# ScalarE alternates exponentials and copies in the wide steps of the second mixer's attention

## The reference

```
score = where(causal, score, -inf);  _, sel = top_k(score, 256)
sc = where(valid, einsum(qa, c_sel), -inf)
p  = softmax(sc);  o_lat = einsum(p, c_sel);  return einsum(o_lat, w_uv)
```

## Time and profile before

| | us |
|---|---|
| median of three runs | 2987.97 |
| lowest, highest | 2983.38, 2990.4 |
| the profiled execution | 2987.91 |
| its span | 2986.1 |
| TensorE busy in it | 2840.4 |
| VectorE busy | 2155.3 |
| ScalarE busy | 1311.8 |
| GpSimd busy | 185.9 |

### The profile page before, as it was taken

The page is one execution under the profiler, slowest core; times in us unless marked ns, Lnnn a source line. Parts: engine busy times, 40 slices in busy tenths (PEclk is TensorE's granted clock), DMA queues, the critical chain, the costliest instruction groups (busy, mean ns, idle before and its releaser), DMA issues.

```text
span 2986.1 us, 37449 instructions
## 1 busy us (share of the span) xinstructions
PE 2840.4 (95%) x13573; PEld 2267.0 (76%) x13573; DVE 2155.3 (72%) x3933; ACT 1311.8 (44%) x2305; POOL 185.9 (6%) x203
## 2 busy tenths in 40 slices
PE   7998997999999999999999999998899899999997
PEld 4885676788888887788888886685567778888886
DVE  7888637988888567766665675998747866665568
ACT  3124744544444554433333442477654433333443
POOL 2050000000000000000000000123520000000000
PEclk9988998999999999999999999999999999999999
DMA  6542033244446773345447762111024244455864
GB/s 229 164 133 38 9 134 120 81 163 162 162 162 208 264 253 113 128 162 162 162 162 283 231 194 74 36 43 34 1 83 137 95 162 162 151 163 186 300 196 147
DMA packets 345414, 436.84 MB, mean 146 GB/s; under 512 B 29685, under 2 KB 191517, under 8 KB 345054
## 3 DMA queue, kind: packets, MB, share of 16 engines
q1 hardware_dynamic: 342274, 428.46, 43.9%
q10 hardware_dynamic: 2956, 5.99, 0.6%
HBM read 317.59 MB, written 116.50 MB: 145 GB/s over the span
## 4 chain that ended last, share of the span: by engine, by line
PE 79%; DVE 13%; ACT 3%; DMA 2%; issue 2%; POOL 1%; SPq 0%; DVEq 0%; ACTq 0%
PE psum L1991 37%; PE psum L1442 21%; PE psum L2865 5%; PE psum L1082 5%; PE psum L1982 3%; DVE count_junk L3375 1%; DMA ada_piece<-in_w_ada 1%; PE psum L4183 1%; PE psum L3055 1%; ACT probs L498 1%; DMA ada_w<-in_w_ada 1%; PE psum L4091 1%; DVE x_t L1688 1%; PE psum L3068 1%; DVE ada_acc L3903 1%
## 5 line engine op out<-in xcount | busy, mean ns | idle before, releaser
L1442 PE MATMUL psum<-far_op,far_op 128*128 128x512 f32 x2772 | 629.4, 389 | 0.0
L1442 PEld LDWEIGHTS psum<-far_op,far_op 128*128 128x128 f32 x2772 | 520.1, 188 | 107.9
L1991 PE MATMUL psum<-x_b,w_near 128*128 128x512 f32 x1440 | 346.2, 389 | 0.8 <-DVE w_near L1614 0.8
L1991 PE MATMUL psum<-x_t,w_near 128*128 128x512 f32 x1440 | 337.1, 389 | 2.3 <-ACT psum L1728 2.3
L1991 PE MATMUL psum<-x_t,w_far 128*128 128x512 f32 x1440 | 336.3, 389 | 0.0
L1991 PEld LDWEIGHTS psum<-x_t,w_near 128*128 128x128 f32 x1440 | 270.0, 188 | 59.6 <-ACT psum L1728 3.6
L1991 PEld LDWEIGHTS psum<-x_b,w_near 128*128 128x128 f32 x1440 | 270.5, 188 | 57.5 <-issue 1.2
L1991 PEld LDWEIGHTS psum<-x_t,w_far 128*128 128x128 f32 x1440 | 270.2, 188 | 56.5 <-ACT u_keep L1740 0.4
L1213 DVE TENSOR_TENSOR far_op<-far_a,far_op 128x512 fp32r<-128x512 f32 x231 | 160.6, 695 | 175.3 <-ACT far_op L1206 173.8
L1206 ACT CAST far_op<-far_a 128x512 fp32r<-128x512 f32 x231 | 143.9, 623 | 315.9 <-PE psum L1442 307.7
L1991 PE MATMUL psum<-x_b,w_far 128*128 128x512 f32 x720 | 176.3, 394 | 9.1 <-DVE val_row L1860 9.1
(11 more groups left out here) (516 smaller groups left out, 4861.3 us busy)
## 6 DMA issues: line engine op xcount, KB each, us to landing
far_a<-row_ops SPq DMA_DIRECT2D x231, 256.0 KB, 2.9
row_ops<-hidden SPq DMA_DIRECT2D x99, 512.0 KB, 5.6
raw<-in_ffn_w SPq DMA_DIRECT2D x88, 512.0 KB, 4.5
col_sums<-hidden SPq DMA_DIRECT2D x66, 512.0 KB, 5.7
far_b<-col_sums SPq DMA_DIRECT2D x132, 256.0 KB, 3.3
raw<-in_w_up SPq DMA_DIRECT2D x44, 512.0 KB, 3.9
hidden<-in_ffn_w SPq DMA_DIRECT2D x44, 512.0 KB, 5.2
far_b<-in_ffn_w SPq DMA_DIRECT2D x66, 256.0 KB, 3.2
```

The source lines that it names most:

```text
L1442: ins = t.matmul(bank(b + n), l[slot][:, rows], r[slot][:], start=(fresh and i == 0 and m == 0), stop=(i == FH - 1 and m == 2), skip_group ...
L1991: ins = t.matmul(bank(b), at[:, l, cols], x[:, k, r], start=(start and k == 0 and m == 0), stop=(k == 3 and m == 2), skip_group_check=not ...
```

## The change

In the loop over the wide steps the exponential of item 2j is put before the copy of item 2j-2. Nothing is added or taken away, and no other engine's list is touched.

```
         for j in range(NARROW, PAIRS2):
+            exponentials(2 * j)
             copy_probs(2 * j - 2)
-            for i in (2 * j, 2 * j + 1):
-                exponentials(i)
+            exponentials(2 * j + 1)
             last_of(j)
             copy_probs(2 * j - 1)
             if j == EARLY_SPLIT:
```

## The result

| | before | changed |
|---|---|---|
| median, us | 2986.40 | 2993.39 |
| lowest, highest, us | 2980.15, 2991.86 | 2990.68, 2997.55 |
| runs | 17 | 17 |
| changed over before | | 1.0026, 95% interval 1.0019 to 1.0032 |
| span of the profiled execution, us | 2986.1 | 2988.9 |

The changed kernel is slower by 0.26%, some 7.8 us of 2986 (5.7 to 9.6 by the interval; the two medians differ by 7.0). The two spans differ by only 2.8 us, less than the ratio says. They are one execution each, and before the change's first effects they already lay apart: the first turn of step 16, ahead of anything that the change can reach, began at 2119.80 us in the one and at 2115.02 in the other. So the traces are compared here over a stretch, from the start of step 17 to the start of the last turn (item 63): 86.37 us before, 93.82 changed, 7.45 more.

A forecast was written before the change was run, and what follows sets the result against it. TensorE's own list was taken to bound an ordinary wide step, with ScalarE having slack. Step terms from -0.5 to +2.3 us summed to 7.65, say +7.6, on 2987.91 us: 2995.5 us, range 2990.0 to 2999.5.

The forecast's parts named there:

- What bounds: An ordinary wide step is as long as TensorE's own list; the first copy has 0.41 us to spare.
- Ordinary steps: First copy late for the second turn: steps 18, 19 +1.4; 22, 23 +1.4; 28 +0.95; 29 +0.7; 30, 31 +1.5 us.
- Steps 20 and 24: Behind VectorE's selection, 0.7 us of delay goes into TensorE's waits for GpSimd of 2.30 and 2.49 us: 0.
- Step 21: Maximum done early, so the first copy is in time, and a 0.46 us wait behind a block's output goes: -0.5 us.
- Steps 16 and 17: Start of the wide steps, where TensorE waits for GpSimd and a copy anyway: -0.1 us together, an estimate.
- Step 25: Second turn late anyway, as TensorE's values took 2.83 us instead of 1.53: 0.
- Steps 26 and 27: Step 27's copy stands behind an exponential held up by VectorE's remainders of the casts: +2.3 us for both steps.
- The clock: A shorter pause after step 24 and a new 3.1 us pause in step 27 were let cancel; bounds -1.4 and +3.
- the rival of a falling clock: Clock falls once or twice more, after step 27's 3.1 us pause; one slow stretch gives 9.2, 2997.1 us; chance 0.20.
- The table: More changes between exponential and copy on ScalarE bring no table load: 0; a load at each would cost 41 us.
- Only half of it arrives: Step 25's slow stretch goes, and recovery at steps 16 to 21 or hidden delays leave about 4.8 us: 2992.7; chance 0.25.
- Faster: Step ends hang on ScalarE's second copy behind two exponentials; relief gives -1.6 us in all, 2986.3; chance 0.05.

The follow-up runs named there:

- the first experiment, wait: Kernel of before, plus a one-column copy waiting for the step's own maximum ahead of each wide step's first copy; 2990.88 us, ratio 1.0014.
- the dose: Kernel of before with VectorE's remainders behind step 27's reciprocals and five one-column copies ahead of each wide step's first copy; 2989.09 us, ratio 1.0008.
- the selection experiment: Kernel of before with the changed order in steps 20, 21, 24 and 25 alone; 2983.51 us, ratio 0.9989.
- not27: Changed kernel, but step 27 keeps the order of before; 2990.09 us, ratio 1.0014 against before.
- rest+: Changed kernel with VectorE's remainders of the casts moved behind step 27's reciprocals; 2989.86 us, ratio 1.0011 against before.
- the seventh experiment: Kernel of before with only VectorE's remainders of the casts moved behind step 27's reciprocals; 2984.14 us, ratio 0.9993.
- shifted: Kernel of before with each wide step's second exponential put behind its second copy; 2989.44 us, ratio 1.0011.

## Why the prediction was right

Forecast 2995.5 us, +7.6, against a ratio that means +7.8, and +7.45 in the traced stretch. The median measured is 2993.39, 2.1 lower than forecast: 1.6 of that is the kernel of before, whose median over 17 runs is 2986.40 and not 2987.97. The mechanism was right, and the terms that belong to it came to 0.1 us in nearly every step. That the sum agrees to some tenths is in part luck: from step 16 on, where the traces differ by 7.64 us, the order of the list accounts for 6.8, and 0.8 us of clock, put at nothing, made up the rest.

- *What bounds.* TensorE's own list, with 0.41 us of cover for the first copy: shown by the first experiment (a copy 0.28 us later costs nothing) and the dose.
- *Ordinary steps.* 0.70 each expected at 640 and 768 keys; 0.67, 0.65, 0.69 and 0.67 measured in 18, 19, 22, 23. At 1024 keys 0.95, 0.7 and 1.5 for 28, 29 and 30 with 31; 0.96, 0.63 and 1.45 measured.
- *Steps 20 and 24.* 0 expected, 0 measured. The second turn came 0.9 us later and the pause for GpSimd was that much shorter, more than the 0.7 I gave, with the same end. These two waits and the ones in step 17 and at the end are why the waits for copies came to 12.1 us and not the 8 to 9 foretold.
- *Step 21.* -0.5 expected, -0.52 measured; the selection experiment shows it by itself.
- *Steps 16 and 17.* -0.1 expected, +0.42 in the changed kernel's trace (10.53 us against 10.11). Behind the slow stretch of step 16 the first turn of step 17 was no longer held up, so that the maximum came 0.10 us behind it, where before it had been 0.24 ahead. The two other kernels with the changed order in these steps, not27 and rest+, ran at the full clock and have 10.00: the -0.1 was right, and about 0.5 is the clock's.
- *Step 25.* 0 expected, -1.57 measured. The 0 held only because the products at the lower clock were to make the second turn late anyway. With the clock up the order itself gains 0.42 here, as in step 21; the other 1.15 are the clock.
- *Steps 26 and 27.* +2.3 expected, 3.65 measured. The mechanism and the pause are as told (3.1 us expected, 3.08 measured; second turn near T+5.7, 5.74 measured). Without the 1.4 us of lower clock behind the pause it is 2.2.
- *The clock.* I had let a gain in step 25 and a loss behind the new pause cancel. Both came, as -1.15 and +1.4, and a third slow stretch in step 16 added 0.5. So the rival of a falling clock was right in its mechanism, and the slow stretch that went away paid for most of it. These are single executions, and the seventh experiment had no slow stretch in step 25 in the old order either; how often each comes in the timed runs is not shown. What this trace shows agrees in kind with the rule of the Trainium skill (TensorE: Matmul & The Clock Gate, HAM oscillation) that gaps between matmuls bring the clock down. But the gaps that this section has in mind are longer than any pause in these steps, so that strictly it did not reach step 27, as the prediction says it did, and it has each gap paid for, where of four pauses of 2.49 us ahead of step 25 one was not.
- *The table.* One table load on the exponentials' line, of 1.28 us, as before. The half of the Trainium skill's rule that counts copy as a member of every set (ScalarE: Activation LUTs, Table sets) holds here: 16 more changes from exponential to copy and as many back brought no load, so batching exponentials apart from copies would have saved none.
- *Only half of it arrives.* The slow stretch in step 25 did go, as this rival says, and the pauses of steps 20 and 24 took up their delays, for which the forecast had already put 0. But no delay of an ordinary step was hidden, and the clock gave back elsewhere what it saved in step 25.
- *Faster.* The waits behind a block's output did go where the rival looked for them; with 0.7 us lost in the steps beside them they did not decide.
- *It reaches the end.* 774.2 and 774.1 us behind the last turn.

## What to carry to other kernels

In an engine's list an instruction that waits for something fresh delays all behind it: what is ready and what the bounding engine needs next comes first, and the fresh item's chain (producer, waiting instruction, copy, hand-over) has to be shorter than the work that covers it. Compute this per step from one timeline; the same swap that loses 0.7 us in a step bound by TensorE costs nothing or gains where a third engine holds it up, so it is worth applying by step and not by loop. A shift of work into an engine already late (VectorE's remainders here) is found by looking at what waits longest in one step, and was worth 1.6 us by itself in the trace.

## What was not expected of the hardware

- The clock behind a pause of TensorE is not settled by the length of the pause to the tenth of a microsecond. In step 25, in the five kernels whose pause ahead of it was about 1.6 us, the 2.4 GHz stayed every time (4.99 to 5.00 us). In the seven with the old order in step 24 the pause was 2.15 to 2.79 us, and step 25 took 6.56 to 6.59 us in five of them and 5.41 and 5.27 in two, where the clock stayed up. Of four pauses of 2.49 us three were followed by the lower clock and one was not.
- The same holds the other way: a pause of 2.02 us in step 27 of the shifted kernel was followed by scores of 3.68 instead of 1.99 us, while in the kernel of before 2.30 us in front of step 21 were not.
- A shorter pause is no safeguard. Behind the same 1.7 us ahead of step 16 the granted clock was 0.57 in three kernels (changed, wait, shifted) and 1.00 in five.
- A copy of one column shows as 0.19 us, but the next instruction of ScalarE starts 0.10 us after it, and five of them take 0.47 us until the next copy starts.
